# A two-layer hybrid decoder trunk on one core: start of the seven-product up projection, way back of x, and last steps of the down projection

## What is computed

```python
h = rmsnorm(x, norm2_g[l]) * (1.0 + sc2) + sh2
u = causal_dwconv(h @ ffn_w_up[l], ffn_conv_w[l], ffn_conv_b[l])
a, b = jnp.split(u, 2, axis=-1)
x = x + g2 * ((jax.nn.silu(a) * b) @ ffn_w_down[l])
```

## Time and profile before

| | us |
|---|---|
| median of 3 runs | 2736.13 |
| lowest, highest | 2733.27, 2743.95 |
| profiled execution | 2744.03 |
| its span | 2742.3 |
| PE busy | 2535.3 (92%) |
| PEld (weight load) busy | 2063.0 (75%) |
| DVE busy | 1444.6 (53%) |
| POOL busy | 1361.8 (50%) |
| ACT busy | 996.6 (36%) |
| mean granted TensorE clock | 0.94 of full speed |

### The profile page before, as it was taken

One profiled execution on the slowest core, in us unless ns is written; L12 is line 12 of the kernel. 1 busy time (PEld: TensorE's weight loads), 2 busy tenths in 40 slices (PEclk: granted clock), 3 DMA queues, 4 the chain that ended last, 5 costly groups with the idle time before them and its releaser, 6 DMA issues. The chain is left out here.

```text
span 2742.3 us, 32812 instructions
## 1 busy us (share of the span) xinstructions
PE 2535.3 (92%) x12414; PEld 2063.0 (75%) x12414; DVE 1444.6 (53%) x1476; ACT 996.6 (36%) x1581; POOL 1361.8 (50%) x802
## 2 busy tenths in 40 slices
PE   4999988998999999999979998889989999999997
PEld 3888656787788888878768875577867888887886
DVE  7553365542756555545455325645365565665543
ACT  3232344431444444333322224434234344442332
POOL 3221792422587777344312139614228777754442
PEclk7999989799999999999989998988989999999998
DMA  6612341022132232554352224301212323326442
GB/s 236 204 46 50 106 124 58 13 77 92 39 95 82 81 93 70 183 167 143 114 204 56 58 61 125 97 31 47 72 59 79 93 75 87 91 87 219 150 146 100
DMA packets 225286, 274.87 MB, mean 100 GB/s; under 512 B 32376, under 2 KB 176605, under 8 KB 223837
## 3 DMA queue, kind: packets, MB, share of 16 engines
q1 hardware_dynamic: 224829, 271.87, 31.8%
q10 hardware_dynamic: 288, 0.79, 0.1%
HBM read 227.80 MB, written 44.04 MB: 99 GB/s over the span
## 5 line engine op out<-in xcount | busy, mean ns | idle before, releaser
L768 POOL TENSOR_TENSOR wLo<-raw,wHi 128x1024 fp32r<-128x1024 f32 x60 | 166.2, 2770 | 606.5 <-ACT wHi L770 604.1
L809 POOL TENSOR_TENSOR downLo<-raw,downHi 128x1024 fp32r<-128x1024 f32 x88 | 213.3, 2426 | 280.6 <-ACT downHi L816 280.6
L1946 DVE TENSOR_TENSOR gateLo<-gateRaw,gateHi 128x512 fp32r<-128x512 f32 x88 | 204.6, 2330 | 212.7 <-ACT gateHi L1559 212.7
L1304 POOL TENSOR_TENSOR prodLo<-comb,prodHi 128x512 fp32r<-128x512 f32 x160 | 220.9, 1386 | 146.8 <-ACT prodHi L802 146.8
L1192 PE MATMUL bank<-gateHi,downHi 128*128 128x512 f32 x704 | 276.9, 393 | 14.6 <-DVE gateLo L1946 14.6
L1192 PE MATMUL bank<-gateHi,downLo 128*128 128x512 f32 x704 | 276.1, 392 | 0.0
L1192 PE MATMUL bank<-gateLo,downHi 128*128 128x512 f32 x704 | 276.0, 392 | 0.0
L828 PE MATMUL bank<-hHi,wHi 128*128 128x512 f32 x768 | 244.1, 400 | 27.7 <-DVE hLo L1668 26.3
L1176 PE MATMUL bank<-tHi,prodHi 128*128 128x512 f32 x640 | 249.7, 390 | 2.6 <-DVE part L1942 2.5
L1176 PE MATMUL bank<-tHi,prodLo 128*128 128x512 f32 x640 | 249.0, 389 | 0.0
L1176 PE MATMUL bank<-tLo,prodHi 128*128 128x512 f32 x640 | 249.0, 389 | 0.0
(11 more groups left out here) (302 smaller groups left out, 5402.7 us busy)
## 6 DMA issues: line engine op xcount, KB each, us to landing
raw<-in_ffn_w_up_dram SPq DMA_DIRECT2D x88, 512.0 KB, 4.6
raw<-in_ffn_w_down_dram SPq DMA_DIRECT2D x88, 512.0 KB, 3.8
raw<-in_ada_w_dram SPq DMA_DIRECT2D x64, 512.0 KB, 3.9
gateOut<-ua SPq DMA_DIRECT2D x44, 512.0 KB, 3.3
gateRaw<-gateOut SPq DMA_DIRECT2D x88, 256.0 KB, 2.7
raw<-in_w_in_dram SPq DMA_DIRECT2D x36, 512.0 KB, 3.8
adaE<-in_ada_w_dram SPq DMA_DIRECT2D x32, 512.0 KB, 9.0
xT<-xtail SPq DMA_DIRECT2D x8, 2048.0 KB, 9.6
```

The costliest lines, as they stand in the source:

```text
L768: eng.tensor_tensor(wLo[slot][:], raw[slot][:], fview(wHi[slot][:]), ALU.subtract).then_inc(s["split_lo"], 1)
L809: eng.tensor_tensor(dwLo[slot][:], raw[kk % 2][:], fview(dwHi[slot][:]), ALU.subtract).then_inc(s["split_lo"], 1)
L1304: pool.tensor_tensor(sLoW[idx][:], product_source(js, idx), fview(sHiW[idx][:]), ALU.subtract).then_inc(s["us_lo"], 1)
L1946: dve.tensor_tensor(dgLo[kk % 4][:], gate_slot(kk)[:], fview(dgHi[kk % 4][:]), ALU.subtract).then_inc(s["g_lo"], 1)
```

## The change

It has three parts.

1. POOL splits products 0 and 1 of the first pair before it makes the combinations. `t_lo` becomes two semaphores, `t_lo_pool` (4 tiles) and `t_lo_dve` (4 tiles). POOL waits only for its own four, PE waits for DVE's before product 2 and for POOL's before product 4, ACT for POOL's before `first_product(0)` and for DVE's before `product_hi` of product 4, and SP for DVE's.
2. SP brings x back in 8 transfers of 512 KB, one after the loads of steps 6, 8, ..., 20.
3. The last two steps (42, 43) run by output tiles instead of the last four.

```diff
-LAST4 = N_DOWN - 4
+LAST2 = N_DOWN - 2
...
@@ sp
-                        sp.wait_ge(s["t_lo"], KT)
+                        sp.wait_ge(s["t_lo_dve"], 4)
...
                 for kk in range(4, N_DOWN):
                     load_gate(kk)
                     load_down(kk)
-                    if kk == 7:
-
-                        sp.wait_ge(s["us_x"], PRODUCTS * (FT - N_STD))
-                        sp.wait_ge(s["params_copied"], 5)
-                        sp.dma_start(xT[:, 0:4, :], xtail[:, 0:4, :]).then_inc(s["x_back"], 16)
-                        sp.dma_start(xT[:, 4:8, :], xtail[:, 4:8, :]).then_inc(s["x_back"], 16)
+                    if kk >= 6 and kk % 2 == 0 and kk < 6 + 2 * KT:
+
+                        if kk == 6:
+                            sp.wait_ge(s["us_x"], PRODUCTS * (FT - N_STD))
+                            sp.wait_ge(s["params_copied"], 5)
+                        m = kk // 2 - 3
+                        sp.dma_start(xT[:, m, :], xtail[:, m, :]).then_inc(s["x_back"], 16)
...
@@ pe
                     if js == 0 and idx == 2:
-                        pe.wait_ge(s["t_lo"], KT)
+                        pe.wait_ge(s["t_lo_dve"], 4)
+                    if js == 0 and idx == 4:
+                        pe.wait_ge(s["t_lo_pool"], 4)
...
-                for kk in range(2, LAST4):
+                for kk in range(2, LAST2):
...
                 for m in range(KT):
-                    for kk in range(LAST4, N_DOWN):
+                    for kk in range(LAST2, N_DOWN):
...
@@ pool
-                pool.wait_ge(s["t_lo"], KT)
+                product_lo(0, 0)
+                product_lo(0, 1)
+                pool.wait_ge(s["t_lo_pool"], 4)
                 for js in range(FT - N_STD):
                     combos(js)
-                    for idx in range(PRODUCTS):
+                    for idx in range(0 if js else 2, PRODUCTS):
                         product_lo(js, idx)
...
@@ act
-                act.wait_ge(s["t_lo"], KT)
+                act.wait_ge(s["t_lo_pool"], 4)
                 for js in range(FT - N_STD):
...
                     first_product(js)
                     if js == 0:
+                        act.wait_ge(s["t_lo_dve"], 4)
                         for idx in range(4, PRODUCTS):
                             product_hi(act, 0, idx)
...
-                used(act, LAST4)
+                used(act, LAST2)
...
@@ dve
-                        dve.wait_ge(s["x_back"], 32)
+                        dve.wait_ge(s["x_back"], 16 * KT)
```

More of the change, by code:

```diff
@@ L558, in build @@
         sd_h sd_sq sd_ss sd_rstd sd_spread sd_rd sd_hi sd_lo
-        x_updated x_saved x_back t_made t_hi t_lo us_hi us_lo us_s us_used us_c us_x
+        x_updated x_saved x_back t_made t_hi t_lo_pool t_lo_dve us_hi us_lo us_s us_used us_c us_x
         up_base up_tap up_silu up_mul g_stored0 g_stored1 gk_loaded0 gk_loaded1 g_hi g_lo dn_used dn_full dn_free""".split()
@@ L582, in used @@
                 eng.wait_ge(s["dn_full"], KT)
-            elif kk < LAST4:
+            elif kk < LAST2:
                 eng.wait_ge(s["dn_used"], kk)
@@ L1307, in t_lo @@
                     pool.wait_ge(s["t_hi"], 2 * kp + 1)
-                    pool.tensor_tensor(tLo[:, kp, :], xT[:, kp, :], fview(tHi[:, kp, :]), ALU.subtract).then_inc(s["t_lo"], 1)
+                    pool.tensor_tensor(tLo[:, kp, :], xT[:, kp, :], fview(tHi[:, kp, :]), ALU.subtract).then_inc(s["t_lo_pool"], 1)
                 for n in range(N_PRE, D0):
@@ L1953, in _ @@
                     dve.wait_ge(s["t_hi"], 2 * kp + 2)
-                    dve.tensor_tensor(tLo[:, 4 + kp, :], xT[:, 4 + kp, :], fview(tHi[:, 4 + kp, :]), ALU.subtract).then_inc(s["t_lo"], 1)
+                    dve.tensor_tensor(tLo[:, 4 + kp, :], xT[:, 4 + kp, :], fview(tHi[:, 4 + kp, :]), ALU.subtract).then_inc(s["t_lo_dve"], 1)
                 gate(0)
```

## The result

| | before | changed |
|---|---|---|
| median, us | 2738.31 (4 runs, 2733.27 to 2743.95) | 2721.93 (4 runs, 2719.06 to 2723.66) |
| ratio | | 0.9935, 95% interval 0.9919 to 0.995 |
| profiled execution, its span | 2744.03, 2742.3 | 2723.66, 2721.9 |
| mean granted clock | 0.940 | 0.942 |

The change is 0.65% faster, which is beyond the 0.5% bound of the prediction, but the time lies 1.9 us above the range (2699 to 2720) and 13.9 us above the forecast. Over all runs, the kernel before has a median of 2740.3 us (51 runs, 2725.7 to 2750.4) and the changed one 2716.3 us (14 runs, 2707.7 to 2723.7). The gain is thus about 24 us, 0.9%: 16.4 us in the four runs of the table, 24.7 and 23.8 us in the two later groups, each against the kernel before in its own group.

The account below looks back on a forecast made before the run. PE, busy 92% of the span, was taken as the bound. 2 x 5.7 + 11.5 + 6.4 - 0.4 = 28.9 us, 28.0 with half a clock loss, off a median of 2736.1 gave 2708 us; range 2699 to 2720.

Parts of the forecast that it names:

- the 0.5% bound: Whole kernel: what a measurement can tell from no change, about 0.5%, 13.7 us.
- through DVE's taps and results, which stay as they are: First products: product 5 follows base(1) by 10.0 us as before, so it starts 5.7 us earlier a layer.
- I take both losses as gone, 11.5 us: Down projection around step 8: x by tiles removes PE's losses of 7.0 us and 4.5 us in the two layers.
- 6.4 for the last steps: Down projection's end: the wait before the last steps goes, 2.3 + 4.1 us over the two layers.
- the price: Last two steps: DVE's two instructions per tile may fall behind PE's results; taken as 0.2 us a layer.
- the half clock loss: Last steps, layer 2: some 1.6 us of the 4.1 lost is clock; half counted, taking 28.9 to 28.0.
- POOL's head start eaten by DVE: First products: overlapped instructions block in full, PE waits 2.4 us before product 2; gain 3.6, total 2712; chance 0.17.
- The tiles still delay the loads: Down projection: eight times a bit late, PE still waits once after step 8; part 2's gain lost, 2719.6; chance 0.09.
- Each tile holds back the odd step's loads: Down projection: odd steps' loads wait until the tile has landed; slower, 2786, or 2746 without clock losses; chance 0.05.
- No change: Whole kernel: PE's time saved is handed back at a later meeting, for instance the layer's end; chance 0.06.

Follow-up runs that it names:

- the two later groups: The changed kernel, unchanged, run again twice: 2716.89 us (4 runs), ratio 0.9906 to the kernel before, and 2714.19 us (6 runs), ratio 0.9908.
- base(1) ahead: Against the changed kernel, ACT's base(1) moved before product 3's high part, silu(1) before the next pair's high parts: 2717.42 us (4 runs).
- the changed kernel again: The changed kernel, unchanged, profiled a second time: 2716.89 us (4 runs), ratio 0.9906 to the kernel before.

## Why the prediction was wrong, point by point

**The direction and the main mechanisms held.** PE doesn't wait before product 0, there is no wait around step 8 and none ahead of the last two steps, and none of the rivals came as it was told. The forecast of the sizes did not hold.

**Part 1: the step that failed is "through DVE's taps and results, which stay as they are".** The first half was right nearly to the tenth. POOL in the changed kernel, with the columns as in the earlier trace rows:

```profile
2048.10 6.54 POOL L1311 TENSOR_TENSOR tLo<-xT,tHi 128x1024 fp32r<-128x1024 f32 x2
2054.61 4.49 POOL L1307 TENSOR_TENSOR prodLo<-raw,prodHi 128x512 fp32r<-128x512 f32 x2
2059.07 2.26 POOL L1298 TENSOR_TENSOR comb<-raw 128x512 f32<-128x512 f32 x1
2061.41 1.29 POOL L1300 TENSOR_TENSOR comb<-comb,raw 128x512 f32<-128x512 f32 x1
...
2065.15 1.27 POOL L1307 TENSOR_TENSOR prodLo<-raw,prodHi 128x512 fp32r<-128x512 f32 x1
```

Three instructions at 2.25 us and four near 1.25, as counted (6.63 + 4.97 us was the sum, 11.78 it became), and product 2 waited 1.94 us where 1.9 was forecast. Base(1) started 6.7 us after the dense stage, forecast 6.5. From there product 5 took 11.2 us (2065.76 to 2076.97) and not 10.0. I had asked whether the next pair's load would be late for POOL and for PE, but not for ACT, whose queue holds the high parts of that pair ahead of the silu. That is 0.94 of the 1.2 us; the other 0.27 is the gate, held longer by POOL. With the silu ahead the wait fell to 0.6. The part saved 4.3 us a layer, not 5.7. In layer 2 some of that went again: behind the wait before product 5 the row at 2078.98 and the next stand 0.43 us apart, the lower of the two clock levels, for about 8 matmuls, 1.6 us. Five executions with this order of the products give ten layers: in three the clock fell there, in three it fell behind product 2's wait instead, and in four not at all. They average 7.6 us for both layers, where 11.4 stood in the sum.

**Parts 2 and 3: mis-sized terms.** "I take both losses as gone, 11.5 us" and 6.4 for the last steps came to 16.6 with the price and the half clock loss deducted. Against that one execution the down projections did lose 18.3 us (502.3 to 484.0). Against six of them it is 2 x 7.4 = 14.8. The waits before step 8 that I priced were 4.32 and 2.86 us, 3.59 on average; the four others were 1.70 to 2.98, 2.27 on average. I halved one clock loss as luck and left the others whole. (Half of the 1.6 us named in part 3 is 0.8 and not the 0.9 taken off; that is 0.1 us of the forecast.) The price of 0.2 us a layer for DVE wasn't due. From the last matmul to the norm's sum it is 2.6 us before and after. DVE's timeline at layer 1's end shows the pairs of instructions 1.36 us apart, at PE's pace:

```profile
1359.88 0.75 DVE L1984 SCALAR_TENSOR_TENSOR xT<-bank,mod,xT 128x512 f32<-128x512 f32 x1
1360.55 0.68 DVE L1647 TENSOR_TENSOR sqn<-sqn,sqn 128x512 f32<-128x512 f32 x1
1361.24 0.75 DVE L1984 SCALAR_TENSOR_TENSOR xT<-bank,mod,xT 128x512 f32<-128x512 f32 x1
```

**The rivals.** *POOL's head start eaten by DVE* gave a wait of 2.4 us before product 2, a fall of the clock behind it, and a gain of 3.6 us a layer. The wait was 1.94. The rival's own time for POOL, 2075.2, would have made it 2.2, so its 2.4 was too high. The clock did fall behind product 2's wait in three of the ten layers, and the gain averaged 3.8 us. That this is close to 3.6 is chance: most of what was missing went at product 5.

The blocking that this rival stood on is real, and here I misread. I took a stretch of 0.97 us beside a gate of 1.21 as partial. But comb0 started 0.16 us behind the gate, when 1.06 us of it were left: it was held for nearly all of that. In the changed kernel DVE's gate above (start 2074.15, 2.16 us) stands between these two rows of POOL:

```profile
2073.95 1.28 POOL L1300 TENSOR_TENSOR comb<-comb,raw 128x512 f32<-128x512 f32 x1
2075.19 2.25 POOL L1301 TENSOR_TENSOR comb<-raw,raw 128x512 f32<-128x512 f32 x1
```

The first ends at 2075.23, the gate 1.08 us later, the second 1.13 us after the gate. They take turns. So it is in the whole trace of the kernel before. All 40 combinations and low parts that started inside a gate or a low part of DVE's ended 1.13 to 1.16 us after it. All 40 gates that started inside an instruction of POOL's ended 1.08 to 1.09 us after that one. Beside DVE instructions with an operand in PSUM, 271 of POOL's took 1.28 to 1.32 us, as with DVE idle (91 of 1.26 to 1.30). The rule of the Trainium skill ("SBUF — State Buffer", "Who interferes with whom") names this pair of instructions and calls the lock exclusive. The trace agrees. My sum came out nearly right all the same, because the row priced at 2.21 us was itself a blocked instruction; full blocking and the forecast were never two different cases.

*The tiles still delay the loads:* no wait at any of the eight steps. The fit of the Trainium skill ("DMA: Bandwidth & Descriptors", "Anatomy of one DMA — SWDGE (gpsimd) path") for transfers from GpSimd would have had a tile in flight for an estimated 3.2 us and PE waiting some 2.4 us a layer. These go out from SP, and no such wait exists. *Each tile holds back the odd step's loads:* excluded in the same way. *No change:* excluded by the pooled runs.

**The baseline and the draw.** The three runs shown had a median of 2736.1; over 51 runs it is 2740.3. The ledger, in us: forecast 2708.1 before rounding; gain too high by 3.8 (part 1) and 1.8 (parts 2 and 3), 2713.7; baseline 4.2 too low, 2717.9; what the pooled difference of 24.0 us has beyond the stages' 22.4, -1.6, gives 2716.3; and the first four runs were 5.6 above that, 2721.9. So 5.6 us of the miss are errors of the working and 8.2 net are differences between executions. The range was too narrow for those: single runs of one kernel spread over 25 us, and I gave 21 for everything together.

## What to carry to other kernels

When an edit brings work forward, walk every in-order queue at the new time, not only the engine that was waited for: here a silu that the forecast left out stood behind instructions that wait for a DMA. Before a stretch beside another engine is called partial, compare it with what was left of that engine's instruction at the start, not with its whole length. Price a wait and the clock loss behind it from several executions, or halve it if there is only one, above all when it is the largest. And compare stages rather than totals: the stages told 0.8 us a layer where 4 to 10 runs of the total could not tell 4 us.

## What the runs showed beyond that

The same untouched stage of 3346 matmuls took 683.1 to 694.2 us over the executions profiled, with 0.91 to 0.89 of the clock granted. This is as much as half of what the whole change brings. The places where the clock is low move about. The two stretches below are a like place in layer 2's mixers, the first in the kernel before and the second in the changed one:

```profile
1800.00:1850.00 50.00, 43.96 (x318) 38.10 (x313) 16.89 (x29) 15.37 (x40) 11.31 (x7) 0.76 0.11 43
```

```profile
1788.00:1838.00 50.00, 43.82 (x298) 38.00 (x294) 16.05 (x28) 14.39 (x35) 11.03 (x7) 0.71 0.12 43
```

With 0.71 of the clock instead of 0.76, PE started 298 matmuls in 50 us and not 318, while being busy for the same 44 us. A busy share doesn't show this loss; the count of instructions in a stretch does.

And what a fall of the clock costs depends on what stands behind it. In the changed kernel again, layer 1, it fell behind product 2's wait for 8 matmuls; PE then came to product 5 without waiting, and the products took 388.1 us, as in layers with no fall (387.9 to 388.2). Where it fell behind product 5's wait, the last one, they took 389.6 to 390.1. The same 1.6 us were free ahead of a wait and paid for behind it. Removing product 5's wait therefore also exposed the loss behind product 2's, and the two are best removed together: in four layers without either of the 1.9 us waits no such stretch of low clock was seen. Four are few: with product 2's wait still there, the two layers with base(1) ahead had none either.
